# A three-layer block kernel: state-space group ends, early rates, and the order of VectorE in the stick-breaking attention

## The reference

```python
def _ssd_scan(x, dt, a_neg, bm, cm):          # 4 groups x 8 heads, chunks of 128 tokens
    cs = jnp.cumsum(a_dt, axis=2)
    decay = jnp.where(causal, jnp.exp(seg), 0.0)
    cb = jnp.einsum('bclgn,bcsgn->bcgls', cc, bc)
    y_diag = jnp.einsum('bcghls,bcsghp->bclghp', cb[:, :, :, None] * decay, xf)
    states = jnp.einsum('bclgn,bclghp->bcghpn', bc, xf * decay_states[..., None])
    y_off = jnp.einsum('bclgn,bcghpn->bclghp', cc, prev) * jnp.exp(cs)[..., None]
    return y_diag + y_off
# then (y + d_skip * x) * silu(z), normalized over each group, times w_out

def short_gated_conv(b_gate, c_gate, u, w_conv):   # three taps
    return b_gate * causal_conv(c_gate * u, w_conv)

def stick_breaking_attention(q, k, v):             # 8 heads of 64
    z = q @ k.T * scale
    log_keep = jnp.where(mask, jax.nn.log_sigmoid(-z), 0.0)
    suffix = lax.cumsum(log_keep, axis=3, reverse=True) - log_keep
    a = jnp.where(mask, jnp.exp(jax.nn.log_sigmoid(z) + suffix), 0.0)
    return a @ v
# then each head's output, and each 64 columns of the convolution's, is normalized by its own mean square
```

## Time and profile before

| | us |
|---|---|
| median of 3 runs | 2809.27 |
| lowest and highest | 2808.86, 2814.31 |
| the profiled execution, whole | 2807.77 |
| its span | 2805.9 |
| TensorE busy in it | 2694.7 |
| VectorE busy | 1523.1 |
| ScalarE busy | 918.7 |
| GpSimd busy | 974.5 |
| mean granted clock of TensorE | 0.992 |

### The profile page before, as it was taken

One profiled execution on the slowest core, in us unless ns is written; L12 is line 12 of the kernel. 1 busy time (PEld: TensorE's weight loads), 2 busy tenths in 40 slices (PEclk: granted clock), 3 DMA queues, 4 the chain that ended last, 5 costly groups with the idle time before them and its releaser, 6 DMA issues.

```text
span 2805.9 us, 31988 instructions
## 1 busy us (share of the span) xinstructions
PE 2694.7 (96%) x12562; PEld 2155.1 (77%) x12562; DVE 1523.1 (54%) x1708; ACT 918.7 (33%) x1159; POOL 974.5 (35%) x1035
## 2 busy tenths in 40 slices
PE   8999989999999999998998999989999999999998
PEld 6877778687777887886766777767888888888886
DVE  6536663778658658668766565565322222222256
ACT  2537771411211212112346666564210001100033
POOL 4533425431431431431422222214433333333342
PEclk9999999999999999999999999999999999999999
DMA  3111003210110110111230000002111111111222
GB/s 131 46 49 31 23 16 108 65 48 21 45 46 16 46 46 23 46 38 38 68 120 23 23 31 30 24 23 90 53 46 52 47 47 52 45 53 45 83 76 75
DMA packets 39894, 139.46 MB, mean 50 GB/s; under 512 B 4352, under 2 KB 4480, under 8 KB 39744
## 3 DMA queue, kind: packets, MB, share of 16 engines
q1 hardware_dynamic: 31392, 110.11, 13.0%
q10 hardware_dynamic: 8352, 27.26, 2.7%
HBM read 124.77 MB, written 12.58 MB: 49 GB/s over the span
## 4 chain that ended last, share of the span: by engine, by line
PE 81%; DVE 11%; ACT 5%; issue 3%; POOL 1%; DMA 0%; DVEq 0%; ACTq 0%; POOLq 0%
PE PS L618 63%; PE PS L979 2%; PE PS L851 2%; PE PS L981 1%; PE PS L967 1%; PE PS L750 1%; PE PS L779 1%; PE PS L986 1%; DVE sb_softplus L2519 1%; PE PS L1293 1%; DVE mla_neg_max L2050 1%; PE PS L1174 1%; DVE sb_z L2498 1%; ACT sb_softplus_hi L1811 1%; PE PS L1135 1%
## 5 line engine op out<-in xcount | busy, mean ns | idle before, releaser
L528 POOL CAST w_hi<-w_stage 128x1024 fp32r<-128x1024 f32 x202 | 219.4, 1086 | 1648.0 <-PE PS L618 1538.3
L531 POOL TENSOR_TENSOR w_lo<-w_stage,w_hi 128x256 fp32r<-128x256 f32 x808 | 707.1, 905 | 16.2
L618 PE MATMUL PS<-XH,w_hi 128*128 128x512 f32 x1408 | 450.1, 401 | 11.3 <-DVE H L1964 3.2
L618 PE MATMUL PS<-XL,w_hi 128*128 128x512 f32 x1408 | 436.7, 392 | 0.0
L618 PE MATMUL PS<-XH,w_lo 128*128 128x512 f32 x1408 | 436.1, 391 | 0.0
L618 PEld LDWEIGHTS PS<-XH,w_hi 128*128 128x128 f32 x1408 | 257.2, 189 | 72.5 <-issue 15.5
L618 PEld LDWEIGHTS PS<-XL,w_hi 128*128 128x128 f32 x1408 | 265.7, 189 | 57.2
L618 PEld LDWEIGHTS PS<-XH,w_lo 128*128 128x128 f32 x1408 | 265.4, 189 | 56.9
L1868 ACT ACTIVATE ffn_t<-ffn_t 128x1024 f32<-128x1024 f32 x32 | 34.0, 1062 | 530.7 <-DVE ffn_t L2573 530.7
L618 PE MATMUL PS<-raw_hi,w_hi 128*128 128x512 f32 x608 | 188.0, 390 | 0.0
L618 PE MATMUL PS<-raw_hi,w_lo 128*128 128x512 f32 x608 | 187.2, 389 | 0.0
(11 more groups left out here) (403 smaller groups left out, 4613.4 us busy)
## 6 DMA issues: line engine op xcount, KB each, us to landing
w_stage<-w SPq DMA_DIRECT2D x202, 512.0 KB, 3.6
pj_kept<-ple_proj_tiles ACTq DMA_DIRECT2D x8, 512.0 KB, 3.0
h_kept<-H ACTq DMA_DIRECT2D x8, 512.0 KB, 3.1
H<-h_kept ACTq DMA_DIRECT2D x4, 1024.0 KB, 5.1
out_t<-out_tiles SPq DMA_DIRECT2D x16, 256.0 KB, 2.1
H<-x_t ACTq DMA_DIRECT2D x3, 1024.0 KB, 11.6
x_again<-x_t ACTq DMA_DIRECT2D x12, 256.0 KB, 3.1
ple_proj_a<-pj_kept ACTq DMA_DIRECT2D x1, 2048.0 KB, 7.8
```

The lines of the kernel that those rows point to most:

```text
L528: nc.gpsimd.tensor_copy(w_hi[:, slot, :, :], w_stage[:, slot, :, :]).then_inc(s_w_hi, 1)
L531: nc.gpsimd.tensor_tensor(w_lo[:, slot, k:k + 2, :], w_stage[:, slot, k:k + 2, :], w_hi[:, slot, k:k + 2, :].bitcast(F32), ALU.subtract).t ...
L618: mm = nc.tensor.matmul(outs[:, half, :], wt[:, slot, k, :], a[:, k - first, half * HB:(half + 1) * HB], start=(k == whole[0] and wt is w_ ...
```

## The change

In the state-space layer, the last transpose of a group goes to bank 4; the rates of a group's first chunk are made before the loop or, for the next group, behind its third convolution tile; in step 7 the skip additions go behind the masking, and in step 8 behind the rows; two z tiles are activated early, and the last one straight from its bank. In the attention, the taps are made one step later, and taps and head scalings stand between the subtraction and the addition; the first adding of parts goes from the end of step 5 to behind the copy of step 6; in the last steps of pass 3, two low parts of heads are made together, ahead of the subtraction.

```diff
--- before.py
+++ after.py
@@ -499,6 +499,9 @@
         def half_place(half, k):
             return SQN[:, k % 2, half_cols(1 - k // 2 % 2 if half else 0)]
 
+        def turned_bank(c):
+            return 4 if c == CHUNKS - 1 else 5
+
         @block.sync
         def _(sp):
             def fetch(n, slot):
@@ -988,10 +991,10 @@
                     c = step - 2
                     if 0 <= c < CHUNKS:
                         pe.wait_ge(s_b, 30 * g + min(4 * c + 4, 30))
-                        if c:
+                        if 0 < c < CHUNKS - 1:
                             pe.wait_ge(s_c, 32 * g + 4 * c)
                         for m in range(4):
-                            mm = nc.tensor.transpose(PS[:, 5, m * P:(m + 1) * P], YR[:, 1, m * P:(m + 1) * P], CN[:, C_ID, :])
+                            mm = nc.tensor.transpose(PS[:, turned_bank(c), m * P:(m + 1) * P], YR[:, 1, m * P:(m + 1) * P], CN[:, C_ID, :])
                         mm.then_inc(s_yt, 1)
                     if step < 9:
                         z_tiles(g, step, 2)
@@ -1626,11 +1629,11 @@
                     if c >= 2:
                         act.wait_ge(s_core, 8 * g + (c - 1))
                     nc.scalar.activation(E[:, c % 2, :, :].rearrange("p (b h) l -> p b (h l)", b=2), PS[:, 6:8, :], ACT.Exp).then_inc(s_ex, 1)
-                raw_z(3, g)
-                for m in range(1, 4):
+                for m in range(1, 3):
                     n = N_CORE - 1 + m
                     act.wait_ge(s_evac[n % 2], (SSD_SLABS // 2) * g + n // 2 + 1)
                     nc.scalar.activation(Z[:, m, :], Z[:, m, :], ACT.Silu).then_inc(s_zs, 1)
+                silu_z(N_CORE + 2, 3, 0, g)
 
             def square(m, g):
                 if m >= 2:
@@ -2262,6 +2265,13 @@
             dve.wait_ge(s_dta, 5)
             dt(v.tensor_tensor(AL[:, :], DTS[:, 1, :], AH[:, :].bitcast(F32), ALU.subtract))
             a_t, b_t, c_t = Tally(dve, s_a), Tally(dve, s_b), Tally(dve, s_c)
+            def rates(g, c):
+
+                for dst, a in ((AVH, AH), (AVL, AL)):
+                    a = a[:, :].bitcast(F32).rearrange("p (c h) -> p c h", h=SSD_HEADS)
+                    v.tensor_tensor(dst[:, :, :], CN[:, C_UPTO, :].unsqueeze(1).to_broadcast([P, HPG, P]),
+                                    a[:, c, bass.ds(g * HPG, HPG)].unsqueeze(2).to_broadcast([P, HPG, P]), ALU.mult).then_inc(s_av, 1)
+
             def group(g):
 
                 def heads(x, c):
@@ -2271,12 +2281,25 @@
                 def by_head(x):
                     return x.rearrange("p (h d) -> p h d", d=PDIM)
 
-                def rates(c):
-
-                    for dst, a in ((AVH, AH), (AVL, AL)):
-                        a = a[:, :].bitcast(F32).rearrange("p (c h) -> p c h", h=SSD_HEADS)
-                        v.tensor_tensor(dst[:, :, :], CN[:, C_UPTO, :].unsqueeze(1).to_broadcast([P, HPG, P]),
-                                        a[:, c, bass.ds(g * HPG, HPG)].unsqueeze(2).to_broadcast([P, HPG, P]), ALU.mult).then_inc(s_av, 1)
+                def skip_and_turned(c):
+                    if c < 0:
+                        return
+                    dve.wait_ge(s_yt, 8 * g + (c + 1))
+                    for m in range(4):
+                        x_c = XS[:, m, c * P:(c + 1) * P]
+                        c_t(v.scalar_tensor_tensor(out=x_c, in0=x_c, scalar=VC[:, bass.ds(g * 4 + (VEC["ssd_d"] + m), 1)],
+                                                   in1=PS[:, turned_bank(c), m * P:(m + 1) * P], op0=ALU.mult, op1=ALU.add))
+
+                def chunk_rows(c):
+                    if c < 0:
+                        return
+                    b_t(v.tensor_tensor(by_head(YR[:, 0, :]), by_head(PS[:, 3, :]), heads(ECS, c), ALU.mult)); b_t.wait()
+                    b_t(v.tensor_tensor(YR[:, 1, :], YR[:, 0, :], PS[:, 2, :], ALU.add))
+
+                def masked(c):
+                    dve.wait_ge(s_ex, 8 * g + (c + 1))
+                    v.tensor_tensor(E[:, c % 2, :, :], E[:, c % 2, :, :], CB[:, :].unsqueeze(1).to_broadcast([P, HPG, P]),
+                                    ALU.mult).then_inc(s_m, 1)
 
                 cv(v.memset(ST[:, :], 0.0)); cv.wait()
                 for step in range(CHUNKS + 2):
@@ -2284,7 +2307,6 @@
                     if c < CHUNKS:
                         if c == 0:
                             dve.wait_ge(s_cs, 6 * g + 6)
-                            rates(0)
                         dve.wait_ge(s_cb, 8 * g + (c + 1))
                         dve.wait_ge(s_bk, 8 * g + (c + 1))
                         if c:
@@ -2296,38 +2318,33 @@
                         if c + 1 < CHUNKS:
                             a_t(v.tensor_tensor(by_head(XFD[:, c % 2, :]), by_head(XF[:, c % 2, :]), heads(DS, c), ALU.mult)); a_t.wait()
                             dve.wait_ge(s_seg, 8 * g + (c + 1))
-                            rates(c + 1)
+                            rates(g, c + 1)
                     c = step - 1
                     if 0 <= c < CHUNKS:
                         dve.wait_ge(s_core, 8 * g + (c + 1))
                     if 0 <= c < CHUNKS - 1:
                         b_t(v.tensor_tensor(by_head(ST[:, :]), by_head(ST[:, :]), heads(DEC, c), ALU.mult)); b_t.wait()
                         b_t(v.tensor_tensor(ST[:, :], ST[:, :], PS[:, 4, :], ALU.add)); b_t.wait()
-                    c = step - 2
-                    if 0 <= c < CHUNKS:
-                        dve.wait_ge(s_yt, 8 * g + (c + 1))
-                        for m in range(4):
-                            x_c = XS[:, m, c * P:(c + 1) * P]
-                            c_t(v.scalar_tensor_tensor(out=x_c, in0=x_c, scalar=VC[:, bass.ds(g * 4 + (VEC["ssd_d"] + m), 1)],
-                                                       in1=PS[:, 5, m * P:(m + 1) * P], op0=ALU.mult, op1=ALU.add))
-                    c = step - 1
-                    if 0 <= c < CHUNKS:
-                        b_t(v.tensor_tensor(by_head(YR[:, 0, :]), by_head(PS[:, 3, :]), heads(ECS, c), ALU.mult)); b_t.wait()
-                        b_t(v.tensor_tensor(YR[:, 1, :], YR[:, 0, :], PS[:, 2, :], ALU.add))
-                    c = step
-                    if c < CHUNKS:
-                        dve.wait_ge(s_ex, 8 * g + (c + 1))
-                        v.tensor_tensor(E[:, c % 2, :, :], E[:, c % 2, :, :], CB[:, :].unsqueeze(1).to_broadcast([P, HPG, P]),
-                                        ALU.mult).then_inc(s_m, 1)
+                    if step < CHUNKS - 1:
+                        skip_and_turned(step - 2)
+                        chunk_rows(step - 1)
+                    elif step <= CHUNKS:
+                        dve.wait_ge(s_yt, 8 * g + (step - 1))
+                        chunk_rows(step - 1)
+                    if step < CHUNKS:
+                        masked(step)
+                    if step >= CHUNKS - 1:
+                        skip_and_turned(step - 2)
                 c_t.wait()
                 rs = E[:, 0, :, :].rearrange("p h l -> p (h l)")
                 sq = (AV[:, :, :].rearrange("p h l -> p (h l)"), E[:, 1, :, :].rearrange("p h l -> p (h l)"))
 
                 def gate(m):
-                    if m == 0:
-                        dve.wait_ge(s_evac[(N_CORE - 1) % 2], (SSD_SLABS // 2) * g + (N_CORE - 1) // 2 + 1)
+                    if m in (0, 3):
+                        n = N_CORE - 1 + m
+                        dve.wait_ge(s_evac[n % 2], (SSD_SLABS // 2) * g + n // 2 + 1)
                     else:
-                        dve.wait_ge(s_zs, 3 * g + m)
+                        dve.wait_ge(s_zs, 2 * g + m)
                     if m >= 2:
                         dve.wait_ge(s_gs, 4 * g + (m - 1))
                         dve.wait_ge(s_gl, 4 * g + (m - 1))
@@ -2395,6 +2412,7 @@
                     dt(v.tensor_scalar(H[:, k, :], H[:, k, :], ALPHA, None, ALU.mult))
             dt.wait()
             dve.wait_ge(s_dta, 7)
+            rates(0, 0)
             with dve.Fori(0, GROUPS - 1) as g:
                 a_t.loop(g, 23), b_t.loop(g, 30), c_t.loop(g, 32), cv.loop(g, 19)
                 group(g)
@@ -2402,7 +2420,9 @@
                 for q in range(2):
                     conv_tile(N_CORE + 3 + q, q, g, g + 1)
                 out_tiles(N_CORE + 5, g)
-                for q in range(2, 6):
+                conv_tile(N_CORE + 9, 2, g, g + 1)
+                rates(g + 1, 0)
+                for q in range(3, 6):
                     conv_tile(N_CORE + 7 + q, q, g, g + 1)
             for tally in (a_t, b_t, c_t, cv):
                 tally.end(GROUPS - 1)
@@ -2496,12 +2516,15 @@
                         if T >= 3:
                             dve.wait_ge(s_o, T - 2)
                         v.tensor_copy(z, PS[:, 0:2, q0:HB]).then_inc(s_zc, 1)
+                    if step == 6:
+                        add_parts(m, 0)
                     if step >= 2:
                         weights_lo(m, step - 2)
                     if m == 3 and step == NU:
```

(23 more changed lines are left out.)

## The result

The changed kernel takes 2786.17 us (median of 4 runs, 2782.9 to 2787.56) where the kernel before takes 2809.16 us in the same session: 0.9916 of it, 95% interval 0.9903 to 0.9929, so 23.0 us less. A second set of runs gave 0.9915.

The account below looks back on a forecast made before the run. TensorE, busy almost throughout, was taken as the bound, so only its waits count. State-space 9.6 us plus attention 16.6 us is 26.2 us: 2809.3 - 26.2 = 2783.1 us; own range 2777 to 2788, 8-in-10 range 2774 to 2795.

Parts of the forecast that it names:

- rival (2): Attention: TensorE's clock stays low after the shorter waits, so 20.5 us gained, 2788.8 us; chance 0.17.
- Rates: State-space part: rates made early end TensorE's wait before the running sums in two groups, 1.7 us each, 3.4 us.
- End orders: State-space group ends: mask wait gone 3.1 us, next slab sooner 1.7 us, first product after the last group sooner 1.4 us.
- The term of the last group: End of the state-space part: earlier activations let the first low part and TensorE's product start sooner, 1.4 us (1.0 to 2.0).
- Pass 0: Attention: 3.3 us fewer waits for low weights plus 2.5 us from full clock, 5.8 us.
- Passes 1 and 2: Attention: three waits of 2.2 us go in each, less 0.15 us for a scaling; 2 x 2.05 = 4.1 us.
- Pass 3: Attention: 9.6 us of waits, 4.3 us stay, 1.8 us come back later, clock returns 3.2 us; 6.7 us gained.
- The signs named ahead: Waits at L967, L979 gone; last transpose under 0.3 us, slab about 0.5 us; L1174 7 to 9 us; attention clock 1.00.
- signs of being wrong: Attention: softplus additions over 1 us after the logarithm, L1152 taking over L1174's waits, or clock near 0.6 behind short waits.
- (1): Attention: the loop itself sets the pace, so only the state-space 9.6 us stays, 2799.7 us; chance 0.10.
- (4): State-space part: running sums wait for something else at the loop's start, 3.4 us lost, 2786.5 us; inside the forecast's 0.62.
- (3): Attention: taps and scalings delay additions fully, 9.4 us slower, 2818.7 us; decided at a mean delay of 0.76 us; chance 0.03.

Follow-up runs that it names:

- e3_rates: Kernel before the change with only the early rates moved, end orders and attention as before: 2807.06 us, 0.9991 of before.
- e2_attn: Kernel before the change with all edits of the attention loop, state-space part as before: 2793.06 us, 0.9941 of before.
- e8_heads_old: Changed kernel with the second of the two low parts of heads put back behind the last subtraction: 2784.93 us.
- e9_gap_load: Changed kernel with two unused VectorE operations added behind each of the 12 taps and 6 scalings, between subtraction and addition: 2797.51 us.

## Why the prediction was right, and where it was off

The direction, the place and the kinds of gain were right; 23.0 us came of 26.2 us. By its number alone rival (2), 2788.8 us, lay nearer to the measured 2786.2 us than the forecast of 2783.1 us; what decides between them is the granted clock of 1.00 in all four passes of both profiles of the changed kernel.

- **Rates**, 3.4 us: 1.8 us in group 1 by the trace, 3.2 us for the edit alone. Right, with the cover named for it; no run shows the 0.1 us that it took off each group for how a start is drawn.
- **End orders**, 3.1 + 1.7 + 1.4 = 6.2 us: 5.7 us. The mask multiplication and the last rows behaved as told, with ScalarE late next at 0.34 us. **The term of the last group was mis-sized**, 0.7 us instead of 1.4 us. The replay let the first low part follow the first high part; in fact VectorE does both gates first (3.09 us from 1315.43) and only at 1318.45 starts the low parts, which took 2.94 us for two instead of 2.48 us:

```profile
1315.43 3.09 DVE L2351 TENSOR_TENSOR ssd_conv<-ssd_x,ssd_z 128x1024 f32<-128x1024 f32 x2
1318.45 2.94 DVE L2355 SCALAR_TENSOR_TENSOR ssd_y_lo<-ssd_conv,VC,ssd_y_hi 128x1024 fp32r<-128x1024 f32 x2
```

- **Pass 0**, 5.8 us: 5.9 us, with the clock at 1.00 as forecast. That the size fits so well is luck. The split was 3.3 us of waits and 2.5 us of clock; in the traces TensorE's idle time in the pass fell from 10.1 to 7.5 us and its busy time, for the same 436 products, from 91.7 to 88.5 us, so 2.6 and 3.3 us. The low weights gave back 3.2 us as replayed, but the waits before a slab product and the running sums grew by 0.6 us, which the replay didn't have. The clock's 0.8 us at the first place is 7 x 0.24 halved, which the second place (4 x 0.43) was not, and no reason was given; unhalved it is 1.7 us. `e3_rates` shows besides that waits and clock are not separate terms: at full clock in that first place, its pass was only 0.5 us shorter. The Trainium skill (TensorE: Matmul & The Clock Gate, "A second HAM failure mode: psum-queue depth-cycling") says that short idles between groups of products can keep the clock cycling; here the parts' 0.96 us beside the 1.16 us before a slab product went with a clock of 0.90, and in the changed kernel, without the 0.96 us, it did not fall. So far the traces agree with the page; but `e3_rates` had both waits at 1.00, and `e2_attn`, without the 0.96 us, fell to 0.94 and 0.87, so these waits alone don't decide it. The second rival, which built on the page, fell for the changed kernel; `e2_attn` shows that it was nearer than its 0.17 suggests.
- **Passes 1 and 2**, 2.05 us each: 1.92 and 1.79 us; 0.45 us of one tap's wait stayed in each.
- **Pass 3**, 6.7 us: 5.0 us. **This is the step that failed**: "By the replay 4.3 us stay ..., 1.8 us come back later", 6.1 us. In the trace 7.9 us stayed at the low weights and L1155 had 2.2 us:

```profile
PE PS L1177 <- DVE sb_weight_lo L2488: 7.9, 5, 3.7
PE PS L1155 <- DVE sb_softplus_lo L2551: 2.2, 3, 1.1
```

The largest is the last, 3.67 us. VectorE ran the low parts of two heads, 1.74 and 1.75 us instead of 1.2 us beside GpSimd, then the subtraction, then a low part of 1.97 us instead of 1.24 us. I had foreseen the order but not the stretching; how much of the 3.67 us is the order's isn't settled, `e8_heads_old` being within scatter. In all, TensorE's idle time in the pass fell by 2.4 us (15.0 to 12.6 us) where the replay had 3.5 us, and the other 2.6 us of the gain are the clock, forecast at 3.2 us.
- **The signs named ahead.** L1174's waits were to fall to 7 to 9 us; they fell to 11.2 us. The replay's own sum was 1.5 + 6.1 = 7.6 us; of the 3.6 us over it 1.8 us are pass 3's, 0.9 us the taps of passes 1 and 2, and 0.8 us mainly a wait early in pass 0 (0.77 us before, 0.75 us after) that the windows of the prediction left out. L1152 did take over 1.7 us. Of the signs of being wrong one came in part: five additions behind scalings started over 1 us after the logarithm, where it cost nothing. The last transposes waited at most 0.31 us (forecast under 0.3 us) and the slab behind them 0.34 us (forecast 0.5 us). The time lay inside the range and the forecast's own range.
- **Rivals.** (1) falls by `e2_attn`, (4) by `e3_rates`. (3) fell because the mean delay was 0.55 us, under its 0.76 us; `e9_gap_load` shows that its price was real, at 0.4 to 0.6 of the size it took.

## What to carry to other kernels

Where two engines pass a tile back and forth, work that is not part of the loop belongs where its engine waits for the other, and what the gap doesn't hold can cost there as well: here 0.4 to 0.6 us for each us once it was used up, and nothing for a lone 1.3 us. Price a clock term as a range that starts at zero, and together with the waits near it: in pass 0, single profiles had 1.6 and 2.0 us for either edit and 5.9 us for both, but 2.7 us for both in `e2_attn`. Before the last step of a loop, look for work of the next stage that is ready already: two parts of the next slab in front of the last wait were worth 2.2 us in the medians.

## What the runs showed of the hardware

Two executions with the same waits of TensorE (1.42 and 1.43 us ahead, then 0.52 and 0.53 us) ran at a granted clock of 0.87 and of 1.00 in matching stretches of 13 us, and pass 0 was 3.1 us apart. The same kernel, profiled twice, was granted 1.00 and 0.66 in matching stretches of 5 us. Why is open. VectorE's low parts of 128x1024 took 1.22 us alone and 1.74 to 2.06 us at the end of pass 3, with GpSimd busy for part or all of each (4.00 of 4 us from 1883 to 1887); the Trainium skill (SBUF — State Buffer, "Who interferes with whom") names that pair, and the trace agrees. The size varies: in the kernel before, one head's low part took 1.23 us with GpSimd busy for nine tenths of it.
